# Merge tiles in other banks, first feed-forward group and adaLN collection in a new order, last two output rows in pieces

## What is computed

```
mod = silu(c) @ ada_w + ada_b                 # six vectors sh1 sc1 gt1 sh2 sc2 gt2
h   = rmsnorm(x, pre_mix_g) * (1 + sc1) + sh1
q_r,k_r,v_r,g_r,q_s,k_s,v_s,a_r,a_s = split(h @ w_in)
ret = silu(g_r) * groupnorm(retention(q_r, k_r, v_r))      # chunkwise, 8 heads
sb  = stick_breaking(q_s, k_s, v_s)                        # causal, 8 heads
y   = (sigmoid(a_r) * (ret @ w_ret) + sigmoid(a_s) * (sb @ w_sb)) @ w_out
x2  = x + gt1 * rmsnorm(y, post_mix_g)
h2  = rmsnorm(x2, pre_ffn_g) * (1 + sc2) + sh2
out = x2 + gt2 * rmsnorm(square(relu(h2 @ w_ff1)) @ w_ff2, post_ffn_g)
```

## Times and profile before

| | us |
|---|---|
| median of 3 runs | 1764.07 |
| their range | 1763.54 to 1768.31 |
| the profiled execution | 1766.35 |
| its span in the trace | 1764.5 |
| PE busy in it | 1708.8 (97%) |

### The profile page before, as it was taken

The page is one execution under the profiler, slowest core; times in us unless marked ns, Lnnn a source line. Parts: engine busy times, 40 slices in busy tenths (PEclk is TensorE's granted clock), DMA queues, the critical chain, the costliest instruction groups (busy, mean ns, idle before and its releaser), DMA issues.

```text
span 1764.5 us, 25435 instructions
## 1 busy us (share of the span) xinstructions
PE 1708.8 (97%) x9968; PEld 1422.3 (81%) x9968; DVE 906.4 (51%) x1284; ACT 560.7 (32%) x949; POOL 602.3 (34%) x256
## 2 busy tenths in 40 slices
PE   4999999999999999999999999899999999999997
PEld 3877877777989898978888997788888888888876
DVE  6757666776456555542113277636261616253526
ACT  4556666110121212120002175333333333323232
POOL 2012111343332322323333742553535353444420
PEclk8999999999999999999999999999999999999999
DMA  9001001255401111113111545111111112020112
GB/s 362 1 25 49 18 32 61 96 203 168 147 28 49 37 40 45 39 42 124 45 46 48 187 160 179 48 48 49 48 59 36 61 35 71 24 85 16 66 77 114
DMA packets 38159, 135.16 MB, mean 77 GB/s; under 512 B 5940, under 2 KB 6836, under 8 KB 37560
## 3 DMA queue, kind: packets, MB, share of 16 engines
q1 hardware_dynamic: 30240, 109.66, 18.3%
q10 hardware_dynamic: 7832, 24.28, 3.7%
HBM read 121.33 MB, written 12.60 MB: 76 GB/s over the span
## 4 chain that ended last, share of the span: by engine, by line
PE 90%; DVE 5%; issue 1%; ACT 1%; DMA 1%; SPq 1%; POOL 0%; POOLq 0%; ACTq 0%; DVEq 0%
PE ps L533 17%; PE ps L531 17%; PE ps L532 16%; PE ps L906 5%; PE ps L908 5%; PE ps L907 5%; PE ps L610 3%; PE ps L611 3%; PE ps L612 3%; PE ps L786 2%; PE ps L663 2%; PE ps L788 2%; PE ps L787 2%; PE ps L627 1%; PE ps L645 1%
## 5 line engine op out<-in xcount | busy, mean ns | idle before, releaser
L438 POOL TENSOR_TENSOR w_hi<-raw,zero 128x1024 fp32r<-128x1024 f32 x58 | 114.3, 1970 | 468.1 <-PE ps L533 272.1
L533 PE MATMUL ps<-r_hi,w_lo 128*128 128x512 f32 x640 | 254.3, 397 | 0.0
L531 PE MATMUL ps<-r_hi,w_hi 128*128 128x512 f32 x640 | 252.2, 394 | 2.1 <-issue 2.1
L532 PE MATMUL ps<-r_lo,w_hi 128*128 128x512 f32 x640 | 252.0, 394 | 0.0
L531 PE MATMUL ps<-w_hi,a_hi 128*128 128x256 f32 x768 | 219.2, 285 | 1.3 <-POOL w_lo L467 0.7
L533 PE MATMUL ps<-w_hi,a_lo 128*128 128x256 f32 x768 | 215.7, 281 | 0.0
L532 PE MATMUL ps<-w_lo,a_hi 128*128 128x256 f32 x768 | 215.5, 281 | 0.0
L472 POOL TENSOR_TENSOR w_lo<-w,w_hi 128x1024 fp32r<-128x1024 f32 x39 | 100.0, 2564 | 221.3 <-ACT w_hi L1222 221.3
L1714 DVE TENSOR_TENSOR m<-m,ps 128x512 f32<-128x512 f32 x208 | 136.4, 683 | 71.2 <-PE ps L908 70.7
L906 PE MATMUL ps<-w_hi,f_hi 128*128 128x512 f32 x392 | 156.2, 398 | 4.8 <-issue 3.7
L907 PE MATMUL ps<-w_lo,f_hi 128*128 128x512 f32 x392 | 156.0, 398 | 0.0
(11 more groups left out here) (232 smaller groups left out, 3427.8 us busy)
## 6 DMA issues: line engine op xcount, KB each, us to landing
raw<-wstream SPq DMA_DIRECT2D x112, 512.0 KB, 3.7
ada_r<-ada_rows SPq DMA_DIRECT2D x32, 512.0 KB, 4.9
w<-wstream SPq DMA_DIRECT2D x32, 512.0 KB, 3.7
ada_s<-ada SPq DMA_DIRECT2D x7, 1024.0 KB, 17.3
m_dram<-m1s ACTq DMA_DIRECT2D x1, 4096.0 KB, 15.6
m<-m_dram ACTq DMA_DIRECT2D x1, 4096.0 KB, 12.2
x_dram<-m ACTq DMA_DIRECT2D x8, 512.0 KB, 4.3
rl_f<-x_dram ACTq DMA_DIRECT2D x2, 2048.0 KB, 10.3
```

What stands on the lines that cost most here:

```text
L438: nc.gpsimd.tensor_tensor(w_hi[:, slot, part], raw[:, h, :], zero[:, 0:1].broadcast_to([P, RAW]), ALU.add).then_inc(w_split, 1)
L531: nc.tensor.matmul(outp, lh, rh, start=(k == 0), stop=False)
L532: nc.tensor.matmul(outp, lh, rl, start=False, stop=False)
L533: last = nc.tensor.matmul(outp, ll, rh, start=False, stop=(k == chunks - 1))
```

## The change

It gives slice 15 to PE and puts 20 and 12 transposes without use of their result between; makes POOL wait for scale1 and shift1 before the low part of piece 1; puts merge tiles into banks 6, 7, 0, 1 (gate) and 4, 5, 2, 3 (branch); in the first feed-forward group reorders ACT's scaling of chunks 8 to 15 against the hidden tiles, puts t4 into y's last row, and moves DVE's evictions of P1 ahead of f_low of P6; and finishes the last rows in pieces.

```diff
-ADA_PE = (2, 10)
+ADA_PE = (2, 10, 15)
+        t4_first = y[:, T - 1, :]
+        y_gain = rh_f[:, 4, :]
+        def gate_bank(j):
+            return ps[:, (6, 7, 0, 1)[j], :]
+        def branch_bank(j):
+            return ps[:, (4, 5, 2, 3)[j], :]
 # sync
-            for t in range(T):
+            for t in range(T - 1):
                 sp.wait_ge(fin_ready, t + 1)
                 sp.dma_start(ov[:, t, :], y[:, t, :]).then_inc(out_done, 16)
+            for d in range(2):
+                sp.wait_ge(fin_ready, T + d)
+                sp.dma_start(ov[:, T - 1, d * HALF:(d + 1) * HALF], y[:, T - 1, d * HALF:(d + 1) * HALF]).then_inc(out_done, 16)
 # gpsimd
+                    if n == 1 and h == 0:
+                        pool.wait_ge(ada_ev, 2)
...
-                add(t4, t2, b21, ALU.subtract).then_inc(ff_t, 1)
+                if first:
+                    pool.wait_ge(n2_x, T)
+                    pool.wait_ge(x2_out, 16 * T)
+                add(t4_first if first else t4, t2, b21, ALU.subtract).then_inc(ff_t, 1)
 # tensor
-                pe.wait_ge(ada_sum, 7 if v == 0 else 14)
+                pe.wait_ge(ada_sum, 7 if v == 0 else 13)
...
+            def keep_busy(n):
+                for q in range(n):
+                    nc.tensor.transpose(ps[:, 1, q % 4 * P:(q % 4 + 1) * P], x_slot(q % 4)[:, 0:P], id_f[:, :])
             ada_summed(0)
             ada_slice(10)
-            ada_summed(1).then_inc(ada_mm, 1)
+            keep_busy(20)
+            ada_summed(1)
+            ada_slice(15).then_inc(ada_mm, 1)
+            keep_busy(12)
...
-            piece_T(PC_MERGE, 0, a_hi, a_lo, lambda j: (ev_dve, EV_MERGE - 3 + j), after=last_r)
+            piece_T(PC_MERGE, 0, a_hi, a_lo, lambda j: None if j < 2 else (ev_dve, EV_MERGE - 5 + j), bank=gate_bank, after=last_r)
             pe.wait_ge(r_lo_done, 4 * RET_G)
-            piece_T(PC_MERGE + 1, 1, r_hi, r_lo, lambda j: None, banks=px)
+            piece_T(PC_MERGE + 1, 1, r_hi, r_lo, lambda j: None if j < 2 else (ev_dve, EV_MERGE - 3 + j), bank=branch_bank)
 # scalar
-            for u in range(8, 16):
-                scale_h2(u)
-            (three row loads, now rows2_loads())
...
                 for j in range(4):
+                    if first and j in (0, 3):
+                        for u in range(8, 12) if j == 0 else range(12, 16):
+                            scale_h2(u)
+                    if first and j == 3:
+                        rows2_loads()
                     hidden(g, order, j)
...
+            for d in range(2):            # last row: two squares of 512, their sum, one root
+                act.wait_ge(ff_ev, FF_EVS * (FF_G - 1) + 2 * T - 1 + d)
+                own(nc.scalar.activation(t4[:, cols], y[:, T - 1, cols], ACT.Square, scale=D ** -0.5, accum_out=tiny[:, 92 + d:93 + d]))
+                if d == 0:
+                    own(nc.scalar.activation(tiny[:, 94:95], tiny[:, 92:93], ACT.Identity, bias=tiny[:, 91:92]))
+            nc.scalar.activation(tiny[:, 15 + T:16 + T], tiny[:, 93:94], ACT.Sqrt, bias=tiny[:, 94:95]).then_inc(fin_root, 1)
 # vector, first group (s2 no longer waits for POOL's low part of P4)
-                dve.wait_ge(ff_wlo, FF_UNITS * g + 4 + P4 + 1)
+                if not first:
+                    dve.wait_ge(ff_wlo, FF_UNITS * g + 4 + P4 + 1)
                 V.tensor_tensor(s2, a22, a21, ALU.subtract).then_inc(ff_s, 1)
                 f_low(P4, a22)
+                if first:
+                    dve.wait_ge(x2_out, 16 * T)
+                    for t in range(4):
+                        evict(P1, t, px[:, t, :], 0, 0, ALU.add, ev)
                 f_low(P6, s2)
 # vector, tail
-                    if d and t:
+                    if 0 < t < T - 1 and d == 0:
                         finish(t - 1)
-                finish(T - 1)
+                    if t == T - 1:
+                        times_gain(d)                 # y_gain half = y half * gtg2 half
+                    if n == 2 * T - 2:
+                        finish_scaled(T - 2)
+                finish_added(T - 2)
+                finish_last()                         # per half: y = y_gain * (1 / root) + x2
```

More of the change, by code:

```diff
@@ L493, in ff_group @@
                 pool.wait_ge(ff_t, 4 * g + 2)
-                add(t4, t2, b21, ALU.subtract).then_inc(ff_t, 1)
+                if first:
+                    pool.wait_ge(n2_x, T)
+                    pool.wait_ge(x2_out, 16 * T)
+                add(t4_first if first else t4, t2, b21, ALU.subtract).then_inc(ff_t, 1)
                 add(b12, b22, b12, ALU.subtract).then_inc(ff_t, 1)
-                low(g, 4 + P4, 1, t4)
+                low(g, 4 + P4, 1, t4_first if first else t4)
                 low(g, 4 + P6, 2, t2)
@@ L534, in tile, with piece_T @@
                 last.then_inc(sem, 1)
-            def piece_T(n, slot, xh, xl, free, banks=pg, chunks=KC, cols=256, order=TT, after=None):
+            def piece_T(n, slot, xh, xl, free, bank=lambda j: pg[:, j % 4, :], chunks=KC, cols=256, order=TT, after=None):
                 pe.wait_ge(w_split, 4 * n + 4)
@@ L541, in piece_T @@
                         pe.wait_ge(*free(j))
-                    tile(banks[:, j % 4, :],
+                    tile(bank(j),
                          lambda k: tuple(w[:, slot, k * cols + m * P:k * cols + (m + 1) * P] for w in (w_hi, w_lo)),
@@ L1210, in _, with rows2_loads @@
             square_x2(7)
[L1211 to L1216 removed]
+            def rows2_loads():
+                act.dma_start(gtg2[:, :], mods[3:4, :].broadcast_to([P, D])).then_inc(rows2_in, 16)
+                act.dma_start(adab2, adab[5:6, :].broadcast_to([P, D])).then_inc(rows2_in, 16)
+                act.dma_start(postg2, postg[1:2, :].broadcast_to([P, D])).then_inc(rows2_in, 16)
             def w_high(slot, src, free, *ready):
@@ L1324, in _ @@
             ff_last(FF_G - 1)
-            for t in range(T):
+            for t in range(T - 1):
                 act.wait_ge(ff_ev, FF_EVS * (FF_G - 1) + 2 * t + 2)
                 root_mean_square(y[:, t, :], tiny[:, t:t + 1], tiny[:, 16 + t:17 + t], fin_root, t4)
+            for d in range(2):
+                cols = slice(d * HALF, (d + 1) * HALF)
+                act.wait_ge(ff_ev, FF_EVS * (FF_G - 1) + 2 * T - 1 + d)
[3 more added lines that the diff above has]
+            nc.scalar.activation(tiny[:, 15 + T:16 + T], tiny[:, 93:94], ACT.Sqrt, bias=tiny[:, 94:95]).then_inc(fin_root, 1)
         @block.vector
@@ L1692, in finish, with times_gain, finish_last @@
                 V.tensor_tensor(y[:, t, :], y[:, t, :], rl_f[:, t, :], ALU.add).then_inc(fin_ready, 1)
+            def finish(t):
+                finish_scaled(t)
+                finish_added(t)
+            def times_gain(d):
+                cols = slice(d * HALF, (d + 1) * HALF)
+                dve.wait_ge(ff_ev, FF_EVS * (FF_G - 1) + 2 * T - 1 + d)
+                V.tensor_tensor(y_gain[:, cols], y[:, T - 1, cols], gtg2[:, cols], ALU.mult).then_inc(fin_gain, 1)
+            def finish_last():
+                dve.wait_ge(fin_root, T)
+                own(V.reciprocal(tiny[:, 31 + T:32 + T], tiny[:, 15 + T:16 + T]))
+                dve.wait_ge(fin_gain, 2)
+                for d in range(2):
+                    cols = slice(d * HALF, (d + 1) * HALF)
+                    V.scalar_tensor_tensor(y[:, T - 1, cols], y_gain[:, cols], tiny[:, 31 + T:32 + T], rl_f[:, T - 1, cols],
+                                           ALU.mult, ALU.add).then_inc(fin_ready, 1)
             def ff_group(g):
```

20 lines of the change are left out of this document (11 added, 9 removed).

## The result

| | before | changed |
|---|---|---|
| median, first pair of series | 1764.38 (1762.98 to 1768.31, 6 runs) | 1750.49 (1747.10 to 1753.57, 6 runs) |
| median, two later pairs | 1764.23; 1764.18 (11 runs each) | 1747.71; 1749.66 (5 runs each) |
| the profiled execution; its span | 1766.35; 1764.5 | 1748.63; 1746.8 |

Ratio 0.9918, 95% interval [0.9907, 0.9929], then 0.9906 [0.9890, 0.9922] and 0.9914 [0.9901, 0.9927]. Against 1764.07 these are 1749.6, 1747.5 and 1748.9 us; the forecast was 1748.5.

A forecast was written before the change was run, and what follows sets the result against it. PE, holding 90% of the chain of waits, bounds the kernel; gains of 2.0 + 4.4 + 7.8 + 1.4 = 15.6 us from the 1764.07 median give 1748.5 us, own range 1746 to 1751, outer ends 1745 and 1755.

The forecast's parts named there:

- Start: adaLN collection and first projection tiles: 2.0 us gained, from +2.8 down to -2.5 where the clock level stays low.
- Merge: First merge tiles: no bank wait, PE starts 3.1 us sooner, no clock fall 1.35 more; 4.4 us, from 3.0 to 4.5.
- First feed-forward group: Reordered ScalarE and VectorE work and moved t4: 2.1 + 3.2 + 1.6 + 1.3 - 0.4 = 7.8 us, bounds 4.2 to 8.4.
- (a): First feed-forward group: ScalarE empties hidden tile 0 before scaling chunks 12 to 15, so PE's 2.1 us wait goes.
- (b): Before P4: with t4 elsewhere s2 runs right after hidden 7; PE waits 0.7 instead of 3.9, 3.2 us gained.
- (c): After the wait before P4: no clock fall to 0.50 for eight matmuls, 1.6 us gained.
- (d): Before P5: P1's evictions ahead of f_low of P6 remove a 1.3 us wait; up to 0.4 comes back at P6.
- rival 3: First feed-forward group: VectorE falls behind POOL, each blocked two-input operation costs 2.1 us; slower, 1768.9 us; chance 0.02.
- Tail: After the last eviction: last rows finished in pieces, half-size last store; 1.4 us gained, from 0.7 to 1.9.
- Rival 1: Start: the transposes don't raise or hold the clock level; start loses 2.5, sum 11.1, 1753.0 us; chance 0.2.
- Rival 2: At P4: POOL gets in first, ahead of f_low; sum 12.0, 1752.1 us; chance 0.15.
- rival 4: Whole change: edits don't do what they say (banks still wait, bigger program, new idle); 1760 to 1764 us; chance 0.03.

## Why the prediction held, point by point

**Sum.** 15.6 forecast; 17.7 between the profiled executions, 13.9, 16.5 and 14.5 between medians. The sum's error is smaller than the spread between executions, so the points tell more than the total. In the first two traces every part came out above its forecast; that the medians lie on both sides of the sum fits the number of low stretches in each execution, which I had not forecast, so the closeness of the total is partly luck.

**Start, 2.0 forecast.** 2.3 between the traces, 2.4 by undoing it: right, and by the mechanism named. In detail it went differently: I had the burst end 0.9 us behind the sums and the high level last through all 32 records and the projection tiles; the burst ended 0.35 us ahead of the sums, the level fell in the middle of the collection, and the second record group took 3.30 us where the first took 1.95. The gain came back at the tiles, where the level rose some five us sooner. POOL's wait, booked at 0.5, seems worth more, since the delay without it also costs an idle PE: the one trace without it lost 2.1.

**Merge, 4.4.** 4.7 and, in another pair, 6.0. The mechanism is as forecast; the upper bound of 4.5 was too low, because it took one low stretch of known length. How long it lasts differs (783 to 786, or 781 to 788), and the bound should have allowed for both.

**First feed-forward group, 7.8.** (a) is 2.1 by undoing it; the other 0.6 of the stage "to P1" is not in my sum: a wait for POOL's `w_lo` went from 0.7 (L467) to 0.2 (L482), and that stage lies anywhere from 320.7 to 321.9 in the twelve traces that have ScalarE's new order. Behind P1 6.1 came where 5.7 was forecast: P4 waits 0.4 instead of 0.7, the clock does not fall. The 4.8 of (b) and (c), 3.2 + 1.6, is what undoing t4 gave. The step that was mis-sized is (d): 1.3 - 0.4 for the place of P1's evictions. Beside the old t4 it is 1.4 (641.5 - 640.1), near enough. With t4 moved, the group depends on it: 7.7 us, more than t4 itself (4.8). The two edits are not a sum, each is worth most with the other in place, and what links them is rival 3's mechanism, VectorE behind POOL. I gave it 0.02 because each product has 5.6 us of cover; two such steps in a row use up 4.4 of it. For the change as it was made the chance was rightly low, for half of it it would have been too low. The Trainium skill, "SBUF — State Buffer", Who interferes with whom, states both halves that these rows show: a step with two inputs from SBUF contends with POOL's reads, one with at most one input there does not, outside certain modes (the copies from PSUM have none).

**Tail, 1.4.** 2.0, just above the upper bound of 1.9. The pieces overlap better than summed: from the start of the last eviction (1739.87) to VectorE's end (1743.94) is 4.1, not 4.4 (the terms listed come to 4.5), and that eviction was not held up.

**Rivals.** Rival 1 fell in the main: the level rises beside transposes alone, and the start gained. But its second half was partly right, for the level did not last through the collection. Rival 2 fell too (f_low of P4 got in after one POOL operation), and rival 4 as well.

## What to carry to other kernels

A wait of PE is worth its length plus what the clock then does, and that second part comes or not from one execution to the next: price it as a range and read it from stages, since medians of four and five runs here hid a 2 us tail. Where VectorE and POOL share the critical stretch, order alone can cost (here 7.7 us for the same operations): put VectorE's PSUM reads beside POOL's operations and avoid two steps with two SBUF inputs in a row there. Before filling an idle slot of PE, ask which buffer it frees earlier, and what the engine that was waiting for that buffer will then run beside.

## What the runs showed that I had not expected

- In the run with 60 of them, float32 transposes alone raised the granted clock (at 36.1) and held it to their end (39.75); matmuls of one column, back to back, let it fall (0.50 from 36.8 in the changed kernel, from 42.9 with 60 transposes).
- The same 1.9 us wait is followed by 0.50 in some executions and by 1.00 in others; at 1.6 us a fall, with mean clocks of 0.992 to 0.996, this fits most of a spread of 7 us.
- VectorE and POOL, both at steps with two inputs from SBUF, take turns: 1.21 became 3.41 and 2.4 became 3.38, in the same rows. VectorE's single-input normalizing steps (SBUF to SBUF) slowed as well, from 5.87 to 9.71 us for sixteen; its copies from PSUM kept their 0.62.
